# The start of a long kernel: inputs laid out in one run per partition, x squared by two engines, scale units before shift units, and ScalarE loads issued later

## The chip, the cores and the metric

The kernel runs on one core of a Trainium2 chip. The metric is the device time of one execution in microseconds, as the median of several. TensorE (PE) multiplies matrices, VectorE (DVE) and ScalarE (ACT) work elementwise, GpSimd (POOL) does a few elementwise steps and indirect transfers, SyncE (SP) issues most loads. Every engine runs its own list of instructions in order, and the lists meet at semaphores.

## The reference

The kernel computes one block of a model with attention, pooling and a mixture of experts, and then two layers of a second model. All is float32, with 512 tokens and a width of 1024. The change touches only the start of the first block:

```python
mod = jax.nn.silu(c) @ w_ada[l] + b_ada[l]               # c: one vector of 1024; w_ada: 1024 x 6144
sh1, sc1, g1, sh2, sc2, g2 = jnp.split(mod, N_MOD, axis=-1)
h = rms_norm(x, norm1_g[l]) * (1.0 + sc1[:, None]) + sh1[:, None]
z = h @ w_in[l]                                          # 1024 x 2048: q, k, v, u
```

So before the first large product there must be the root mean square of every token of x, the scale `sc1` and the shift `sh1`, and these two are products of one vector with the first 2048 columns of `w_ada`. Later come attention on q, k, v, window means (2, 4, 8, 16 wide) of u, and the experts.

## The kernel before

Nothing is planned by a compiler: each engine's list is written out by hand, and `take(engine, semaphore)` waits for a semaphore and clears it. Arrays are kept transposed, 128 channels on the partitions and 512 tokens along them, so x and h are 8 tiles of 128x512.

**Loads.** SP issues x (one transfer, 1024 rows of 2 KB) and then "units" of 2 MB into a ring of six slots (L1888 to L1891). A unit is 512 columns of a weight matrix with all 1024 rows, so it too is 1024 rows of 2 KB. Their order is w_ada 0, 1, 2, 3 (0 and 1 hold the shift, 2 and 3 the scale), w_in, w_ada 4, 5, w_in, w_ada 6, 7, and so on. A slot is refilled once its unit is used up. ACT issues the small parameters (`params_loaded`, L2329 to L2332) at the very start: a vector table, the constants, and a row broadcast to all partitions. After the fourth w_ada unit it issues the late constants, pool_w and the two router matrices (L2367 to L2370). POOL issues the inverse counts of the window means, `invcnt` (L1941), when all q and k are rotated (`qk_ready` 8).

**Mean square.** ACT squares the 8 tiles of x into two buffers `sq` in turn (L2343). PE sums each over its partitions with a product with ones (`sumsq`, L2040) and frees the buffer. ACT then takes the inverse root: a logarithm and an exponential, each with a table load (L2348, L2351).

**Scale and shift.** `mod_products` (L2057) makes the row of a w_ada unit: 8 products with a 32-column stationary tile, four of them side by side. ACT copies the row out of PSUM (`mod_moved`, L2357), and `mod_columns` (L2067) turns it into columns with four products of one moving column each, into bank 7. PE's list is: products 0, products 1, columns 0, products 2, columns 1, products 3, columns 2, columns 3. The w_ada units 4 to 11 are multiplied by DVE instead (`mod_unit`, L2604 and L2606), and PE turns them by `mod_columns` between the products of the projections.

**h and the projections.** DVE adds the bias (L2581), makes the gain (L2587, L2588) and scales x into hT (`normed`, L2593). ACT adds the shift tile by tile (L2374, semaphore `h_ready`). PE starts the first product of w_in (L2091) on the first tile. The projections of q and k (L2091), u (L2103) and v (L2115) follow without a pause. ACT copies each result (L2381, L2384, L2394, L2401), and DVE rotates q and k (L2616 to L2618), with a `mod_unit` after every second one. Then DVE waits for `invcnt` and makes the window means (L2629 to L2635) and `mod_unit` 8 to 11. PE needs the means at L2125, and w_ada unit 8 turned after the second product of v.

Of the kernel before, what the change touches and what calls it, by code (L numbers as in the profile page):

```python
# [17 lines left out]
ALU = mybir.AluOpType  # L18
# [3 lines left out]
P = 128  # L22
T = 512
D = 1024
# [18 lines left out]
POOL_W = (2, 4, 8, 16)  # L43
POOL_PAD = 8


P1 = {}
def _cols(table, spec):
# [40 lines left out]
def take(eng, sem, value=1):  # L89

    eng.wait_ge(sem, value)
    eng.sem_clear(sem)
# [39 lines left out]
        self.n = 0  # L132


def build(nc, xT_d, zero_row, par1, row1, cn, invcnt, w_ada, w_in, w_pool, w_out, w_rg, w_re, w_gate, w_up, w_down,
          w2, out):
    ctx = ExitStack()
    with ctx:
# [20 lines left out]
        for late, early in (("slot_full6", "wa_full"), ("slot_full7", "bonus_full"), ("slot_free6", "kr_full"),  # L159
                            ("slot_free7", "mla_q_full"), ("raw_tiles", "sg_full0"), ("tiles_used", "sg_full1")):  # L160
            sems[late] = sem(early)
        first_only = ("silu_c", "raw_ready", "v_ready", "u_ready", "qk_ready", "mix_ready", "x_mixed", "router_loaded",
                      "pool_w_loaded", "scores_done", "pooled", "params_loaded", "choices_full", "h_stored", "h_ready",
                      "x_loaded", "y_stored", "routed", "y_summed", "mod_ready", "rs_ready", "scaled", "pad_zero")
        for late, early in zip(("g_rk_full0", "g_rk_full1", "g_uw_free0", "g_uw_free1", "r_in_full", "r_bt_full", "r_k_free",
                                "r_bn_full", "r_k_done", "r_tok_full", "r_km_full", "r_func_full", "r_args_full", "r_sw_full",
                                "r_sa_full", "ring_free", "kk_full", "g_w_done", "x_tiles", "g_e_in0", "g_e_in1", "g_pt_full0",
# [141 lines left out]


        def ada_unit(n):
            return w_ada[0, :, n * 512:(n + 1) * 512].rearrange("(k p) n -> p k n", p=P)
        def in_unit(n):
            return w_in[0, :, n * 512:(n + 1) * 512].rearrange("(k p) n -> p k n", p=P)
        def out_unit(n):
            return w_out[0, :, n * 512:(n + 1) * 512].rearrange("(k p) n -> p k n", p=P)
        units = [ada_unit(n) for n in range(4)]
        ada_at, in_at = list(range(4)), []
        for n in range(4):
            in_at.append(len(units))  # L320
            ada_at += [len(units) + 1, len(units) + 2]
# [6 lines left out]
        def slot(n, k=8):  # L328
            return ring[:, n % SLOTS, :].rearrange("p (k n) -> p k n", k=k)
# [1555 lines left out]

        @block.sync
        def _(sp):
            sp.dma_start(xT[:], xT_d.rearrange("(k p) t -> p k t", p=P)).then_inc(sem("x_loaded"), 16)  # L1888
            for n, u in enumerate(units):
                take(sp, slot_free[n % SLOTS])  # L1890
                sp.dma_start(slot(n), u).then_inc(slot_full[n % SLOTS], 16)  # L1891
# [141 lines left out]
        def _(pe):  # L2033
# [26 lines left out]
            def mod_columns(u):  # L2060

                take(pe, sem(f"wT_full{u % 2}"))
                if u % 4 == 0:
                    take(pe, bank_free[7])
                for m in range(4):
                    col = 4 * (u % 4) + m
                    mm = pe.matmul(bank[7][:, col:col + 1], mod_rows[:, u % 2, m * P:(m + 1) * P],  # L2067
                                   quarters if u < 4 else ones[:, 0:1], start=True, stop=True)
                if u % 4 == 3:
                    mm.then_inc(for_dve[7], 1)  # L2070
                elif u >= 4:
                    mm.then_inc(sem(f"wT_free{u % 2}"), 1)

            sumsq(1, KD, 0)
            for u in range(4):
                mod_products(u)
                if u > 0:
                    mod_columns(u - 1)
            mod_columns(3)

            for n in range(2):
                s = in_at[n] % SLOTS
# [244 lines left out]
        def _(act):  # L2327
# [11 lines left out]
            def squares(src, tiles, n0=0):  # L2339
                for i in range(tiles):  # L2340
                    j = (n0 + i) % 2
                    take(act, sem(f"sq_free{j}"))
                    act.activation(sq[:, j, :], src(i), ACT.Square).then_inc(sem(f"sq_full{j}"), 1)  # L2343
# [15 lines left out]
                act.sem_inc(slot_free[ada_at[u] % SLOTS], 1)  # L2359
                act.sem_inc(sem(f"wT_full{u % 2}"), 1)  # L2360

            act.wait_ge(sem("x_loaded"), 16)
            squares(lambda i: xT[:, i, :], KD)
            inverse_root(1, 1.0 / D)
            for u in range(4):
                mod_moved(u)
            act.dma_start(c_sb[:, late_cols:], cn[:, late_cols:]).then_inc(sem("pool_w_loaded"), 16)  # L2367
            act.dma_start(pool_w[:], w_pool[0].rearrange("g c d -> c g d")).then_inc(sem("pool_w_loaded"), 16)
            act.dma_start(w_router[:, :, 0:4], w_rg[0].rearrange("(k p) n -> p k n", p=P)).then_inc(sem("router_loaded"), 16)
            act.dma_start(w_router[:, :, 4:36], w_re[0].rearrange("(k p) n -> p k n", p=P)).then_inc(sem("router_loaded"), 16)  # L2370
            act.wait_ge(sem("mod_ready"), 1)
            for k in range(KD):
                act.wait_ge(sem("scaled"), k + 1)
                act.activation(hT[:, k, :], hT[:, k, :], ACT.Identity, bias=mod[:, k:k + 1]).then_inc(sem("h_ready"), 1)  # L2374
            for i in range(8):
# [12 lines left out]
                if i % 4 == 3:  # L2388
                    act.sem_inc(slot_free[in_at[i // 4] % SLOTS], 1)
# [175 lines left out]
        def _(dve):  # L2565
# [8 lines left out]
            chain(dve.tensor_tensor(small[:, 20:21], small[:, 18:19], small[:, 19:20], ALU.subtract))  # L2574
            chain(dve.tensor_scalar(small[:, 21:22], small[:, 20:21], 0.2, None, ALU.add))
            chain(dve.tensor_scalar(subln, par("subln_g"), 0.8, None, ALU.mult))

            def modulation(first, b):
                take(dve, for_dve[b])
# [16 lines left out]
            def mod_unit(u):  # L2596
# [9 lines left out]
                        chain(dve.scalar_tensor_tensor(row, w, small[:, k:k + 1], row, ALU.mult, ALU.add))  # L2606
                dve.sem_inc(slot_free[s], 1)
                dve.sem_inc(sem(f"wT_full{u % 2}"), 1)
            modulation(0, 7)
            gains(0, par("norm1_g", 0, 8))  # L2610
            normed(0, 1)
            for i in range(8):
                dve.wait_ge(sem("raw_ready"), i + 1)
                if i == 0:
                    dve.wait_ge(sem("pool_w_loaded"), 32)
                chain(dve.tensor_tensor(qkT[:, i, :], raw[:, i % 2, :], const("cosA"), ALU.mult))  # L2616
                chain(dve.tensor_tensor(rtmp[:, i % 2, :], rot_raw[:, i % 2, :], const("sinA"), ALU.mult))
                dve.tensor_tensor(qkT[:, i, :], qkT[:, i, :], rtmp[:, i % 2, :], ALU.add).then_inc(sem("qk_ready"), 1)  # L2618
                if i % 2 == 1:
                    mod_unit(4 + i // 2)  # L2620
# [23 lines left out]
            dve.wait_ge(sem("router_loaded"), 32)  # L2644
# [437 lines left out]
```

## Time and profile before

| | us |
|---|---|
| median of 3 runs | 1996.08 (1995.02 to 1997.31) |
| profiled execution: span from first to last instruction | 2001.2 |
| PE busy | 1764.2 (88%) |
| DVE busy | 857.6 (43%) |
| ACT busy | 592.7 (30%) |

The profile page gives the profiled execution by its span, 2001.2 us, and no other time of it. The timed runs are other executions. All starts below are microseconds from the first instruction of the profiled execution. Float32 products show as two records each. A row of a timeline merges equal instructions that follow each other; what stands in brackets is the idle time before it and what ended it. Engine names with a q (ACTq, SPq) are the queue side of an engine: issued transfers and semaphore steps.

### The profile page before, as it was taken

The numbers are of one execution on the slowest core, as the hardware profiler recorded it, in microseconds if no ns is written. First come the engines' busy times: TensorE is split into PE (matmuls) and PEld (weight loads), VectorE is DVE, ScalarE is ACT, GpSimd is POOL, SyncE is SP. The second block draws the span as 40 slices with busy tenths as digits, with TensorE's granted clock in tenths as the row PEclk, the third lists the DMA queues.
The fourth block names the chain that finished last, engine by engine and source line by source line (L and its number), as shares of the span: only waits on it lengthen the run. The fifth ranks groups of instructions, "written<-read, shape, count | busy, mean of one in ns | idle before, by whom it ended". The sixth has DMA issues, their size and how long they took to land.

```text
span 2001.2 us, 44027 instructions
## 1 busy us (share of the span) xinstructions
PE 1764.2 (88%) x17970; PEld 1033.3 (52%) x17970; DVE 857.6 (43%) x1514; ACT 592.7 (30%) x1018; POOL 243.5 (12%) x270
## 2 busy tenths in 40 slices
PE   5998895977778877898999899999989998899996
PEld 2444543544444444445865784354447856853452
DVE  1567524111111111367666753151457747642331
ACT  3314521000000000334324424252253325424442
POOL 0002211111111111006112100001002103000001
PEclk8998996999999999998999999999999999999998
DMA  9758025999999999521000003110211000012101
GB/s 358 259 197 291 1 69 220 370 423 424 423 424 424 425 424 413 216 74 33 3 3 2 3 20 109 42 43 32 80 43 35 3 2 2 4 65 104 42 1 42
DMA packets 75098, 307.75 MB, mean 154 GB/s; under 512 B 10908, under 2 KB 22300, under 8 KB 57888
## 3 DMA queue, kind: packets, MB, share of 16 engines
q1 hardware_dynamic: 63280, 291.98, 37.2%
q0 software_dynamic: 5360, 9.33, 1.3%
q10 hardware_dynamic: 6272, 3.81, 0.6%
q8 instruction: 135, 2.21, 0.5%
q14 instruction: 51, 0.42, 0.1%
HBM read 301.01 MB, written 16.52 MB: 159 GB/s over the span
## 4 chain that ended last, share of the span: by engine, by line
PE 73%; DVE 13%; another core or an unknown queue 6%; ACT 4%; issue 3%; DMA 1%; DVEq 0%; ACTq 0%; POOL 0%; POOLq 0%
PE bank L2253 12%; PE bank L496 12%; PE bank L2269 6%; PE bank L1027 6%; PE bank L525 5%; PE bank L532 4%; PE bank L2091 3%; PE bank L2175 3%; PE bank L998 2%; DVE arena L1596 2%; ACT arena L1039 1%; PE bank L512 1%; PE bank L2115 1%; PE bank L2103 1%
## 5 line engine op out<-in xcount | busy, mean ns | idle before, releaser
L496 PE MATMUL bank<-hT,arena 128*128 128x512 f32 (+1 forms) x640 | 287.7, 605 | 3.6 <-ACTq L1040 2.4
L2253 PE MATMUL bank<-arena 128*64 128x256 f32 x1792 | 216.3, 399 | 66.9 <-remote 66.9
L525 PE MATMUL bank<-arena 64*64 64x64 f32 x6656 | 215.5, 220 | 22.7 <-DVE arena L1726 7.2
L525 PEld LDWEIGHTS bank<-arena 64*64 64x64 f32 x6656 | 203.8, 136 | 37.0 <-DVE arena L1726 10.1
L2253 PEld LDWEIGHTS bank<-arena 128*64 128x64 f32 x1792 | 135.6, 143 | 158.0 <-issue 107.8
L496 PEld LDWEIGHTS bank<-hT,arena 128*128 128x128 f32 (+1 forms) x640 | 122.9, 194 | 161.2 <-issue 156.6
L2859 DVE COPY arena<-bank 128x256 f32<-128x256 f32 x32 | 13.6, 425 | 329.6 <-PE bank L2261 329.6
L2269 PE MATMUL bank<-arena 128*64 128x512 f32 x448 | 104.0, 606 | 16.4 <-remote 16.4
L1027 PE MATMUL bank<-arena 128*128 128x512 f32 x256 | 110.4, 593 | 0.0
L1039 ACT ACTIVATE arena<-bank 128x512 f32<-128x512 f32 (+2 forms) x124 | 73.2, 590 | 118.9 <-PE bank L496 79.2
L532 PE MATMUL bank<-hT,arena 128*128 128x512 f32 x224 | 105.0, 607 | 1.7 <-remote 1.7
L2513 ACT ACTIVATE arena<-bank 128x512 f32<-128x512 f32 x32 | 19.1, 597 | 292.8 <-PE bank L2269 292.8
L1027 PEld LDWEIGHTS bank<-arena 128*128 128x128 f32 x256 | 48.5, 190 | 60.6 <-issue 60.1
L1852 DVE TENSOR_REDUCE arena<-bank 128x1 f32<-128x512 f32 x48 | 33.2, 692 | 106.0 <-PE bank L998 104.7
L2506 ACT ACTIVATE arena<-bank 128x256 f32<-128x256 f32 x32 | 12.3, 383 | 187.7 <-remote 187.7
L2269 PEld LDWEIGHTS bank<-arena 128*64 128x64 f32 x448 | 31.0, 138 | 69.7 <-issue 69.7
L512 PE MATMUL bank<-c_sb,arena 128*128 128x128 f32 x352 | 54.1, 288 | 12.8 <-ACTq L1040 7.9
L2091 PE MATMUL bank<-hT,arena 128*128 128x512 f32 x128 | 58.6, 619 | 5.3 <-ACT hT L2374 5.3
L532 PEld LDWEIGHTS bank<-hT,arena 128*128 128x128 f32 x224 | 39.8, 189 | 42.9 <-issue 41.2
L1986 POOL DMA_INDIRECT y_scratch<-arena x31 | 31.7, 1024 | 226.6 <-remote 205.9
L1176 ACT ACTIVATE arena<-bank 128x512 f32<-128x512 f32 x60 | 35.4, 597 | 80.2 <-PE bank L525 78.4
L512 PEld LDWEIGHTS bank<-c_sb,arena 128*128 128x128 f32 x352 | 40.4, 145 | 36.2 <-issue 36.0
(448 smaller groups left out, 2677.1 us busy)
## 6 DMA issues: line engine op xcount, KB each, us to landing
arena<-w_gate SPq DMA_DIRECT2D x28, 2048.0 KB, 30.6
arena<-w_up SPq DMA_DIRECT2D x28, 2048.0 KB, 21.0
arena<-w_down SPq DMA_DIRECT2D x28, 2048.0 KB, 26.2
arena<-w_ada SPq DMA_DIRECT2D x12, 2048.0 KB, 19.7
arena<-w_in SPq DMA_DIRECT2D x10, 2048.0 KB, 11.7
arena<-w_out SPq DMA_DIRECT2D x6, 2048.0 KB, 7.6
arena<-w_in SPq DMA_DIRECT2D x6, 1536.0 KB, 6.9
hT<-w_up SPq DMA_DIRECT2D x4, 2048.0 KB, 20.9
```

The source lines that it names most:

```text
L496: m = pe.matmul(bank[b][0:w, :], slot2(n)[:, k, c:c + w], hT[:, k, :], start=(k == 0), stop=(k == KD - 1))
L512: m = pe.transpose(bank[b][:, ts(t)], src[:, ts(t)], ident)
L525: m = pe.matmul(o[half(f), s, t], lhs[half(f), s, t], rhs[half(f), s, t], start=True, stop=True)
L532: m = pe.matmul(bank[b][:, :], slot2(3 + PLACE[i] // 4)[:, k, (PLACE[i] % 4) * P:(PLACE[i] % 4 + 1) * P], hT[:, k, :], start=(k == 0), sto ...
L998: pe.matmul(bank[i % 4][:, :], m_q[0:QK_M, h, ts(q)], m_k[0:QK_M, h, :], start=True, stop=True).then_inc(for_dve[i % 4], 1)
L1027: m = pe.matmul(bank[b][:, :], slot2(n)[:, k, (m_ % 4) * P:(m_ % 4 + 1) * P], mix[:, k, :], start=(i == 0), stop=(i == KD - 1))
L1039: chain(act.activation(dst, src, func, **kw))
L1596: dve.copy_predicated(blocks(g_T[d]), merged(d, l, False), blocks(bank[2 + d])).then_inc(sem(f"g_t_full{d}"), 1)
L2091: mm = pe.matmul(bank[b][:, :], slot(s)[:, k, m * P:(m + 1) * P], hT[:, k, :], start=(k == 0), stop=(k == KD - 1))
L2175: mm = pe.matmul(bank[4 + i % 4][:, :], slot(out_at + i // 4)[:, k, (i % 4) * P:(i % 4 + 1) * P], mixT[:, k, :], start=(n == 0), stop=(n = ...
L2253: mm = pe.matmul(bank[b][c * CAP:(c + 1) * CAP, 0:FE // 2], XT[j][:, k % 4, k // 4, :], e_slot(e_at(e, i), KD)[:, k, c * (FE // 2):(c + 1) ...
L2269: mm = pe.matmul(bank[6 + j][c * CAP:(c + 1) * CAP, :], hidT[:, j, f % 2, f // 2, :], e_slot(e_at(e, 2), 4)[:, f, c * HALF:(c + 1) * HALF] ...
```

## The change

- The host lays x out as two halves of 4 tiles, and each w_ada, w_in and w_out unit as one run of 16 KB per partition. pool_w and the router matrices (now one matrix) are also contiguous per partition. x is loaded in two transfers with a semaphore each.
- The first four units are w_ada 2, 3, 0, 1.
- ACT squares the even tiles of x into `sq` 0, DVE the odd ones into `sq` 1.
- PE's list is: products 2, columns 2, products 3, columns 3 (into bank 4), three products of ones with constants into bank 7 (`keep_busy`), products 0, columns 0, products 1, columns 1 (bank 7).
- DVE takes the scale from bank 4, makes the gains and hT, and then takes the shift from bank 7. ACT waits for both (`mod_ready` 2).
- ACT's transfers of late constants, pool_w and router stand behind its shift of h.

```diff
-        units = [ada_unit(n) for n in range(4)]
-        ada_at, in_at = list(range(4)), []
+        units = [ada_unit(n) for n in SCALE_FIRST]          # SCALE_FIRST = (2, 3, 0, 1)
+        ada_at, in_at = [SCALE_FIRST.index(n) for n in range(4)], []
...
-            sp.dma_start(xT[:], xT_d.rearrange("(k p) t -> p k t", p=P)).then_inc(sem("x_loaded"), 16)
+            for half in range(2):
+                sp.dma_start(xT[:, 4 * half:4 * half + 4, :], xT_d[half]).then_inc(sem(f"x_loaded{half}"), 16)
...
+            def keep_busy(n):
+
+                pe.wait_ge(bank_free[7], 1)
+                for _ in range(n):
+                    pe.matmul(bank[7][:, :], ones, c_sb[:, 0:512], start=True, stop=True)
             sumsq(1, KD, 0)
-            for u in range(4):
+            for u in SCALE_FIRST[:2]:
                 mod_products(u)
-                if u > 0:
-                    mod_columns(u - 1)
-            mod_columns(3)
+                mod_columns(u)
+            keep_busy(3)
+            for u in SCALE_FIRST[2:]:
+                mod_products(u)
+                mod_columns(u)
...
-            act.wait_ge(sem("x_loaded"), 16)
-            squares(lambda i: xT[:, i, :], KD)
+            for i in range(0, KD, 2):
+                if i % 4 == 0:
+                    act.wait_ge(sem(f"x_loaded{i // 4}"), 16)
+                take(act, sem("sq_free0"))
+                act.activation(sq[:, 0, :], xT[:, i, :], ACT.Square).then_inc(sem("sq_full0"), 1)
             inverse_root(1, 1.0 / D)
-            for u in range(4):
+            for u in SCALE_FIRST:
                 mod_moved(u)
-            act.dma_start(...)   # four transfers, two of them the router's
-            act.wait_ge(sem("mod_ready"), 1)
+            act.wait_ge(sem("mod_ready"), 2)
             for k in range(KD):
                 act.wait_ge(sem("scaled"), k + 1)
                 act.activation(hT[:, k, :], hT[:, k, :], ACT.Identity, bias=mod[:, k:k + 1]).then_inc(sem("h_ready"), 1)
+            act.dma_start(...)   # three transfers, one of them the router's
...
+            for i in range(1, KD, 2):
+                if i % 4 == 1:
+                    dve.wait_ge(sem(f"x_loaded{i // 4}"), 16)
+                take(dve, sem("sq_free1"))
+                dve.tensor_tensor(sq[:, 1, :], xT[:, i, :], xT[:, i, :], ALU.mult).then_inc(sem("sq_full1"), 1)
...
-            modulation(0, 7)
+            take(dve, for_dve[4])
+            chain(dve.tensor_tensor(mod[:, 8:16], bank[4][:, 8:16], par("b_ada", 8, 8), ALU.add))
+            dve.sem_inc(bank_free[4], 1)
+            dve.sem_inc(sem("mod_ready"), 1)
             gains(0, par("norm1_g", 0, 8))
             normed(0, 1)
+            shift_moved()        # the same for mod[:, 0:8] from bank 7
```

## Rows read from the trace of the kernel before

**Rows 1.** The page: busy time by engine.
```profile
PE 1764.2 (88%) x17970; PEld 1033.3 (52%) x17970; DVE 857.6 (43%) x1514; ACT 592.7 (30%) x1018; POOL 243.5 (12%) x270
```

**Rows 2.** The chain of waits, 0 to 60 us: start, length, what.
```profile
0.74 10.93 DMA xT<-xT_in
...
13.41 9.85 PE bank L2040 x16
23.26 3.57 PE bank L2057 x32
...
29.44 1.85 PE bank L2057 x16
...
36.67 3.52 PE bank L2067 x16
...
41.22 3.41 DVE hT L2593 x5
...
44.66 0.73 ACT hT L2374
...
45.44 14.77 PE bank L2091 x27
```

**Rows 3.** ACT's timeline, 5 to 45 us: start, length, instruction, idle before.
```profile
10.53 0.21 ACT L2334 ACTIVATE small<-p 128x8 f32<-128x8 f32 x1 [7.07 <-DMA r<-row]
...
20.26 0.63 ACT L2343 ACTIVATE sq<-xT 128x512 f32<-128x512 f32 x1 [0.30 <-PE bank L2040]
...
27.36 0.58 ACT L2357 ACTIVATE arena<-bank 128x512 f32<-128x512 f32 x1
...
31.45 0.60 ACT L2357 ACTIVATE arena<-bank 128x512 f32<-128x512 f32 x1 [2.58 <-PE bank L2057]
...
39.05 5.51 ACTq L2370 DMA_DIRECT2D w_router<-w_re  x1
```

**Rows 4.** PE's timeline, 28 to 48 us.
```profile
28.39 1.05 PE L2067 MATMUL bank<-c_sb,arena 128*128 128x1 f32 x8 [1.56 <-remote]
...
33.62 3.05 PE L2057 MATMUL bank<-arena,small 128*32 128x512 f32 x16 [1.34 <-remote]
```

**Rows 5.** Stretches: length, then busy time by engine, granted clock, DMA.
```profile
30.80:34.20 3.40, 2.06 (x24) 1.26 (x20) 0.00 (x0) 0.60 (x1) 0.00 (x0) 1.00 1.05 387
34.30:51.30 17.00, 11.74 (x35) 6.24 (x28) 5.90 (x11) 5.61 (x9) 0.00 (x0) 0.50 1.07 377
...
171.40:174.00 2.60, 0.00 (x0) 0.00 (x0) 2.42 (x5) 0.78 (x2) 0.00 (x0) 1.00 1.08 317
174.20:184.30 10.10, 9.44 (x22) 3.74 (x22) 7.23 (x15) 6.13 (x16) 4.68 (x3) 0.50 0.99 411
```

**Rows 6.** PE's timeline, 103 to 175 us.
```profile
127.48 7.11 PE L2103 MATMUL bank<-hT,arena 128*128 128x512 f32 x16
...
148.16 0.95 PE L2067 MATMUL bank<-c_sb,arena 128*128 128x1 f32 x8
```

**Rows 7.** DMA queues (q1 SP's, q10 ACT's), 47 to 53 us: packets, MB, share of 16 engines.
```profile
q1 hardware_dynamic: 1033, 2.08, 97.5%
q10 hardware_dynamic: 1036, 0.03, 12.5%
```

**Rows 8.** The same, 357 to 358.9 us, expert weights alone, 16 KB per packet.
```profile
q1 hardware_dynamic: 46, 0.75, 96.3%
```

**Rows 9.** The same, 114 to 121 us (q0 is POOL's).
```profile
q0 software_dynamic: 319, 1.05, 45.0%
```

**Rows 10.** DVE's timeline, 56 to 186 us.
```profile
65.67 0.69 DVE L2616 TENSOR_TENSOR arena<-arena,c_sb 128x512 f32<-128x512 f32 x1 [4.72 <-ACTq L2387]
...
121.71 0.71 DVE L2629 TENSOR_TENSOR arena<-arena 128x527 f32<-128x527 f32 x1 [5.00 <-DMA arena<-invcnt]
...
135.53 0.71 DVE L2629 TENSOR_TENSOR arena<-arena 128x527 f32<-128x527 f32 x1 [3.65 <-ACTq L2396]
...
141.74 5.47 DVE L2606 SCALAR_TENSOR_TENSOR arena<-arena,small 128x512 f32<-128x512 f32 x7
```

More of the change, by code:

```diff
@@ L44 @@
 POOL_PAD = 8
+SCALE_FIRST = (2, 3, 0, 1)
 P1 = {}
@@ L132, in reset, with build @@
         self.n = 0
-def build(nc, xT_d, zero_row, par1, row1, cn, invcnt, w_ada, w_in, w_pool, w_out, w_rg, w_re, w_gate, w_up, w_down,
+def build(nc, xT_d, zero_row, par1, row1, cn, invcnt, w_ada, w_in, w_pool, w_out, w_r, w_gate, w_up, w_down,
           w2, out):
@@ L161, in build @@
             sems[late] = sem(early)
-        first_only = ("silu_c", "raw_ready", "v_ready", "u_ready", "qk_ready", "mix_ready", "x_mixed", "router_loaded",
+        first_only = ("silu_c", "raw_ready", "x_loaded1", "u_ready", "qk_ready", "mix_ready", "x_mixed", "router_loaded",
                       "pool_w_loaded", "scores_done", "pooled", "params_loaded", "choices_full", "h_stored", "h_ready",
-                      "x_loaded", "y_stored", "routed", "y_summed", "mod_ready", "rs_ready", "scaled", "pad_zero")
+                      "x_loaded0", "y_stored", "routed", "y_summed", "mod_ready", "rs_ready", "scaled", "pad_zero")
         for late, early in zip(("g_rk_full0", "g_rk_full1", "g_uw_free0", "g_uw_free1", "r_in_full", "r_bt_full", "r_k_free",
@@ L311, in ada_unit @@
         def ada_unit(n):
-            return w_ada[0, :, n * 512:(n + 1) * 512].rearrange("(k p) n -> p k n", p=P)
+            return w_ada[n]
         def in_unit(n):
-            return w_in[0, :, n * 512:(n + 1) * 512].rearrange("(k p) n -> p k n", p=P)
+            return w_in[n]
         def out_unit(n):
-            return w_out[0, :, n * 512:(n + 1) * 512].rearrange("(k p) n -> p k n", p=P)
-        units = [ada_unit(n) for n in range(4)]
-        ada_at, in_at = list(range(4)), []
+            return w_out[n]
+        units = [ada_unit(n) for n in SCALE_FIRST]
+        ada_at, in_at = [SCALE_FIRST.index(n) for n in range(4)], []
         for n in range(4):
@@ L1887, in _ @@
         def _(sp):
-            sp.dma_start(xT[:], xT_d.rearrange("(k p) t -> p k t", p=P)).then_inc(sem("x_loaded"), 16)
+            for half in range(2):
+                sp.dma_start(xT[:, 4 * half:4 * half + 4, :], xT_d[half]).then_inc(sem(f"x_loaded{half}"), 16)
             for n, u in enumerate(units):
                 take(sp, slot_free[n % SLOTS])
-                sp.dma_start(slot(n), u).then_inc(slot_full[n % SLOTS], 16)
+                sp.dma_start(ring[:, n % SLOTS, :], u).then_inc(slot_full[n % SLOTS], 16)
             sp.dma_start(y_d, zero_row.to_broadcast([2 * T, D])).then_inc(sem("y_loaded"), 16)
@@ L2062, in mod_columns @@
                 take(pe, sem(f"wT_full{u % 2}"))
-                if u % 4 == 0:
-                    take(pe, bank_free[7])
+                b = 4 if u in SCALE_FIRST[:2] else 7
+                if u % 4 == 0 or u == SCALE_FIRST[0]:
+                    take(pe, bank_free[b])
                 for m in range(4):
                     col = 4 * (u % 4) + m
-                    mm = pe.matmul(bank[7][:, col:col + 1], mod_rows[:, u % 2, m * P:(m + 1) * P],
+                    mm = pe.matmul(bank[b][:, col:col + 1], mod_rows[:, u % 2, m * P:(m + 1) * P],
                                    quarters if u < 4 else ones[:, 0:1], start=True, stop=True)
-                if u % 4 == 3:
-                    mm.then_inc(for_dve[7], 1)
+                if u % 4 == 3 or u == SCALE_FIRST[3]:
+                    mm.then_inc(for_dve[b], 1)
                 elif u >= 4:
                     mm.then_inc(sem(f"wT_free{u % 2}"), 1)
+            def keep_busy(n):
+                pe.wait_ge(bank_free[7], 1)
+                for _ in range(n):
+                    pe.matmul(bank[7][:, :], ones, c_sb[:, 0:512], start=True, stop=True)
             sumsq(1, KD, 0)
-            for u in range(4):
+            for u in SCALE_FIRST[:2]:
                 mod_products(u)
-                if u > 0:
-                    mod_columns(u - 1)
-            mod_columns(3)
+                mod_columns(u)
[3 more added lines that the diff above has]
+                mod_columns(u)
             for n in range(2):
@@ L2360, in mod_moved @@
                 act.sem_inc(sem(f"wT_full{u % 2}"), 1)
-            act.wait_ge(sem("x_loaded"), 16)
-            squares(lambda i: xT[:, i, :], KD)
+            for i in range(0, KD, 2):
[3 more added lines that the diff above has]
+                act.activation(sq[:, 0, :], xT[:, i, :], ACT.Square).then_inc(sem("sq_full0"), 1)
             inverse_root(1, 1.0 / D)
-            for u in range(4):
+            for u in SCALE_FIRST:
                 mod_moved(u)
[L2367 to L2370, printed above, removed]
-            act.wait_ge(sem("mod_ready"), 1)
+            act.wait_ge(sem("mod_ready"), 2)
             for k in range(KD):
@@ L2374, in _ @@
                 act.activation(hT[:, k, :], hT[:, k, :], ACT.Identity, bias=mod[:, k:k + 1]).then_inc(sem("h_ready"), 1)
+            act.dma_start(c_sb[:, late_cols:], cn[:, late_cols:]).then_inc(sem("pool_w_loaded"), 16)
+            act.dma_start(pool_w[:], w_pool).then_inc(sem("pool_w_loaded"), 16)
+            act.dma_start(w_router[:], w_r).then_inc(sem("router_loaded"), 16)
             for i in range(8):
@@ L2608, in mod_unit, with shift_moved @@
                 dve.sem_inc(sem(f"wT_full{u % 2}"), 1)
-            modulation(0, 7)
+            take(dve, for_dve[4])
+            chain(dve.tensor_tensor(mod[:, 8:16], bank[4][:, 8:16], par("b_ada", 8, 8), ALU.add))
+            dve.sem_inc(bank_free[4], 1)
+            dve.sem_inc(sem("mod_ready"), 1)
             gains(0, par("norm1_g", 0, 8))
+            def shift_moved():
+                take(dve, for_dve[7])
+                chain(dve.tensor_tensor(mod[:, 0:8], bank[7][:, 0:8], par("b_ada", 0, 8), ALU.add))
+                dve.sem_inc(bank_free[7], 1)
+                dve.sem_inc(sem("mod_ready"), 1)
             normed(0, 1)
+            shift_moved()
             for i in range(8):
@@ L2643, in _ @@
             gains(1, par("norm2_g", 0, 8))
-            dve.wait_ge(sem("router_loaded"), 32)
+            dve.wait_ge(sem("router_loaded"), 16)
             def over_cols(v):
@@ L3070, in col, with by_units @@
         return np.asarray(a).reshape(-1, P).T
+    def by_units(w):
+        w = np.asarray(w)[0]
+        return w.reshape(KD, P, -1, 512).transpose(2, 1, 0, 3).reshape(-1, P, KD * 512)
     par1 = np.concatenate([col(norm1_g), col(b_ada), col(norm2_g), col(final_g), col(pool_scale), col(subln_g), col(c),
@@ L3076 @@
     out = nc.dram_tensor("out", (D, T), F32, kind="ExternalOutput").ap()
-    build(nc, put("xT_in", np.asarray(x)[0].T), put("zero_row", np.zeros((1, D), np.float32)), put("par1", par1), put("row1", row1), put("cn", cn), put("invcnt", ic),
-          put("w_ada", w_ada), put("w_in", np.asarray(w_in)[..., rotary_columns()]), put("w_pool", w_pool), put("w_out", w_out), put("w_rg", w_router_group),
-          put("w_re", w_router_expert), put("w_gate", w_gate), put("w_up", w_up), put("w_down", w_down), second_inputs({**rest, "final_norm_g_2": final_norm_g_2}, put), out)
+    build(nc, put("xT_in", np.asarray(x)[0].T.reshape(2, 4, P, T).transpose(0, 2, 1, 3)), put("zero_row", np.zeros((1, D), np.float32)), put("par1", par1), put("row1", row1), put("cn", cn), put("invcnt", ic),
+          put("w_ada", by_units(w_ada)), put("w_in", by_units(np.asarray(w_in)[..., rotary_columns()])),
+          put("w_pool", np.asarray(w_pool)[0].transpose(1, 0, 2)), put("w_out", by_units(w_out)),
+          put("w_route", np.concatenate([np.asarray(w_router_group)[0], np.asarray(w_router_expert)[0]], axis=1).reshape(KD, P, 36).transpose(1, 0, 2)),
+          put("w_gate", w_gate), put("w_up", w_up), put("w_down", w_down), second_inputs({**rest, "final_norm_g_2": final_norm_g_2}, put), out)
     r = run_bass_kernel_spmd(nc, [arrays], core_ids=[0])
```

## The prediction

> **What bounds the kernel now.** I read the page first, then the chain of waits of the first 60 us, then the timelines of PE, ACT and DVE there, the stretches with their granted clock, and last the DMA queues. The page shows PE as the bound: it is busy for 88% of the span [rows 1]. The change touches the stretch before PE's long run, so what counts is when the first projection starts and how fast it then goes. The chain shows what that start hangs on: x arrives at 11.67, the sums of squares run from 13.41 to 23.26, products and columns of the four w_ada units end at 40.19, and the projection starts at 45.44 [rows 2]. Two of these pieces are not what they seem. The wait for x is not the last one: ACT and DVE are held until the broadcast row of parameters lands at 10.53, and from there to ACT's first square it is 2.1 us of small work [rows 3]; x has come by then. And from 40.39 on the last link is ACT's own list. It issues the router matrix for 5.51 us, until 44.56, and can only then add the shift [rows 3], though DVE had the first tile ready at about 42.0 (it began its tiles at 41.22, five in 3.41 us [rows 2]). The clock is the third piece: PE ran at 1.2 GHz from 34.3 to 51.3 (granted 0.50), after a stretch in which it was busy for 2.06 of 3.40 us, half of this with one-column products [rows 4, 5].
>
> **Parameters: 0 us.** Packets of 16 KB of the expert weights took 1.9 x 16 x 0.963 / 46 = 0.64 us each [rows 8]. Where SP's and ACT's queues were both full, they sent packet for packet: 1033 against 1036 [rows 7]. The constants and the row are 128 pieces each, 16 per DMA engine, so after the change they go in turn with sixteen packets of 8 or 16 KB. With 8 KB at half of 0.64 and small ones at 0.1 that is 13 x 0.42 + 3 x 0.74 = 7.7 us from about 3 us on, landing at 10.7 against 10.53. If they start before x they land near 9 (-1.5); if mostly behind 16 KB packets, 3 us later. I take 0. x itself, with 16 packets per engine, still is not last.
>
> The Trainium skill (DMA: Bandwidth & Descriptors, Queues, rings and completion order) says that a DMA engine drains a whole packet of some 9 to 17 descriptors from one ring before it turns to the next. By that rule the row would wait for about one packet of x and land near 9.5, and the stall priced below for `invcnt` would shrink to under 1 us. The near equal counts in [rows 7] speak for one by one, and I go by them.
>
> **Squares: 0 us.** ACT needs 0.63 us a tile, PE 0.86, so ACT was not the limit. Each of the two buffers goes round: PE's product, release, square, product. ACT's idle 0.30 us, ended by PE [rows 3], is this round, and it stays with DVE as the second squarer: its elementwise product of 512 columns takes 0.69 us [rows 10], 0.06 more. I bound it by half a us on both sides. So sums end at 23.3 as before.
>
> **New order of units: +0.2 us if the clock stays full.** From the end of the sums to the first columns PE must wait for ACT's inverse root, with its two table loads, and one copy: 28.39 - 23.26 = 5.13 us [rows 2, 4]. Before, two products filled 3.6 of it; now only one does, as the columns stand ahead of the second product. One unit in the new order is products 1.85 [rows 2], end of products to copy 0.15, copy 0.60 [rows 3], copy to columns 0.45 (27.94 to 28.39), columns 1.05 [rows 4]: 4.1 us with nothing beside it. So columns of the fourth unit end at 23.26 + 5.13 + 1.05 + 3 x 4.1 = 41.7, and the three products of `keep_busy` add 3 x 0.86 = 2.6 (a 16-record group of eight takes 7.0 to 7.1 us [rows 6], 0.87 each). From 44.3 it is 1.3 us to the projection (DVE's add, semaphores, ACT's 0.73 tile): 45.6 against 45.44. The scaling of x, 5.4 us of DVE, lies beside the shift's units and goes off the path; the w_ada units arrive ahead of need, which removes the 1.34 us wait at 33.62 [rows 4], and ACT's 5.51 us issue is gone. All of it is paid back by the serial order. ACT's moved transfers are three instead of four and are queued behind the shift, ahead of its copies of q. The late constants are what DVE's first rotation needs, 13 us after the start of the projection; the shift is done 5 us after that start and they land at worst 10 us later, 8 turns of 0.64 + 0.17 us for them and as many for pool_w. The 2 us that this may be late are covered by the 4.72 us that DVE was idle before its second rotation [rows 10]; without it they would be paid.
>
> **The clock in the new order: +4.9 us.** After products of the first unit PE now stands idle for about 3.3 us, then does one-column work. Rows show twice what follows: at 30.8 to 34.2 PE was busy for 2.06 us with the clock full, then it fell; at 171.4 to 174.0 it was idle, then it fell for 10 us [rows 5]. I expect it to fall by 28 us. At 1.2 GHz the 16 one-column products took 3.52 us instead of 2.1 [rows 2], so 0.75 more per unit; products 1.85 more; `keep_busy` 2.6 more. It rose again at 51.3 after the projection had run for 5.9 us [rows 5], so `keep_busy` mostly raises it only at its own end. Second unit 1.85 + 0.75, `keep_busy` 2.6 less 0.3 for an early rise: 4.9, and the projection starts at 50.5. Bounds: 0 if it never falls; if it stays low to the end, two more units, 4 x 1.3 = 5.2 more (10.4).
>
> **The clock in the projection: -1.0 us.** Before, 45.44 to 51.3 ran at half speed, a loss of 2.9 us [rows 5]. After `keep_busy` come again two units with pauses, so I expect a low clock near the start, but a shorter one. Ends: 0 and -2.9.
>
> **invcnt: +1.7 us.** POOL's 256 pieces of 4 KB were sent between 114 and 121 [rows 9], beside three 2 MB units in 2 KB packets. Now these units are 24 packets of 0.64 us per DMA engine, issued at 108.8 and running until 126; POOL's 16 per engine go in turn with them, 16 x (0.64 + 0.17) = 13 us from 114.5: landing near 128 instead of 121.7. DVE waits for them (5.00 us before, some 6.3 more). It then has 3.65 us of waiting for ACT that absorb it [rows 10], so the last window mean and `mod_unit` 8 come some 2.6 us later. That one ended at 147.2, PE needed it at 148.16 [rows 6, 10]: 0.9 us of slack, so PE loses 1.7. Ends: 0 (it is sent before the big packets) and +3.
>
> **Sum.** 0 + 0 + 0.2 + 4.9 - 1.0 + 1.7 = +5.8 us. The later stages shift as a whole: expert weights wait for free slots, which free with the work. The sum is against the profiled span, 2001.2, which lies 5.1 above the median of the runs; carried over as a difference it gives 1996.1 + 5.8 = 2001.9. All lower ends together: -1.5 - 0.5 + 0.2 - 2.9 = -4.7; all upper: 3 + 0.5 + 0.2 + 10.4 + 0 + 3 = +17, which needs everything at once.
>
> **The rivals.** (a) As forecast, 0.52: +2.5 to +9. (b) The other side: the clock is full through the units and in the projection, 0.20. Its place is the pause after the first products; its price is all of the 4.9 and the 2.9 that the projection lost before: 0.2 - 2.9 + 1.7 = -1.0, 1995.1, with 2 us to either side. It decides if the projection starts before about 47 with a granted clock of 1.00. For it: PE's pauses up to 30.8 left the clock full, and it came back at 184.3 after scattered work of attention [rows 5]. Against: this pause is longer than any of these. (c) Small transfers do not go one by one behind the large ones, 0.15: the parameters land 1 us earlier and `invcnt` costs nothing, 5.8 - 1 - 1.7 = +3.1, 1999.2. For it: nothing here shows 16 KB packets beside ACT's queue. Against: [rows 7]. It is what the rule of the Trainium skill named above would bring. (d) The parameters are stuck behind 16 KB packets, 0.13: 5.8 + 3 = +8.8, 2004.9, seen as a first square near 15.7 instead of 12.65. For it: the large transfers are issued within microseconds of each other. Against: p, constants and row are issued as early.
>
> **Chances.** Within 0.2% is within 4 us, about what a measurement of this kernel can tell from no change. Slower by more: 0.39 of (a), 0.04 of (c), all of (d): 0.56. Same: 0.13 of (a), 0.11 of (b), 0.09 of (c): 0.33. Faster: 0.09 of (b), if it comes with less than the stall for `invcnt`, and 0.02 of (c): 0.11. The range 1994.5 to 2006.5 takes in (c), two thirds of (b) and most of (d); outside lie about 0.08 below and 0.10 above.
>
> **What would show it.** In the changed profile: the first square near 12.7; ACT and DVE idle before squares, ended by PE; PE idle for 3 us after the first products; a granted clock of 0.50 from about 28 to 40; the projection's start near 50; the wait for `invcnt` at 10 us or more; a PE wait of 1 to 2 us at the columns of unit 8. I am wrong if the projection starts before 46, or if the clock is full through the units.

## The result: 1% slower, and where the 20 us went

| | before | after |
|---|---|---|
| median, us (4 runs each) | 1996.22 | 2015.78 (2014.5 to 2018.28) |
| ratio, 95% interval | | 1.0104 (1.0082 to 1.0125) |
| span of the profiled execution, us | 2001.2 | 2012.7 |

The direction was forecast, the size was not: +5.8 us (2001.9) were expected and +19.6 us came, 9 us above the upper end of the range (2006.5). One execution of the kernel before, among those run beside the experiments below, took 9078 us and is left out.

The spans differ by 11.5 us only. That is an accident of the two profiled executions. The stages behind the second attention scores are the same code, but took 1827.1 us before and 1819.0 after, and the one of before ran longer at half clock (from 200 us on its mean granted clock is 0.97, that of after 0.98). The view of cores shows the mean over the whole span, first of before, then of after:

```profile
core 0: 2001.2 us, clock 0.964
```

```profile
core 0: 2012.7 us, clock 0.971
```

So I compare stage by stage, up to the second group of attention scores, which both kernels reach by the same path. Before it started at 174.07 (the end of the idle stretch in [rows 5]), after at 193.74: 19.7 us later, which is the measured difference. From PE's timelines, first the start of the v product and of these scores before, then the scores after:

```profile
134.43 13.90 PE L2115 MATMUL bank<-arena,hT 128*128 128x512 f32 x32
174.07 5.35 PE L2137 MATMUL bank<-arena 64*128 64x512 f32 x8 [2.69 <-ACTq L2424]
```

```profile
193.74 5.07 PE L2148 MATMUL bank<-arena 64*128 64x512 f32 x8 [3.07 <-ACTq L2437]
```

Now the chain of waits of the kernel after, 0 to 70 us, which answers to [rows 2]:

```profile
1.67 13.83 DMA r<-row
...
18.41 9.59 PE bank L2043 x14
...
28.04 1.12 PE bank L2043 x2
29.16 1.85 PE bank L2060 x16
31.01 3.19 another core or an unknown queue
...
34.29 1.86 PE bank L2071 x8
36.15 3.65 PE bank L2060 x16
...
40.80 1.86 PE bank L2071 x8
42.66 5.33 PE bank L2082 x6
47.99 1.85 PE bank L2060 x16
...
57.35 12.69 PE bank L2102 x25
```

The chain now begins with the broadcast row instead of x. PE's pause of 3.19 us after the first products is plain to see, and behind it columns take 1.86 us, products 3.65 and `keep_busy` 5.33: all at half clock. The stretches show the clock itself (length, busy time by engine, granted clock, DMA):

```profile
24.10:34.10 10.00, 6.87 (x26) 1.61 (x24) 1.39 (x2) 5.59 (x7) 0.00 (x0) 1.00 0.99 424
34.30:47.80 13.50, 12.42 (x38) 5.91 (x38) 4.69 (x10) 0.60 (x1) 0.00 (x0) 0.50 1.00 427
48.00:58.00 10.00, 6.44 (x50) 3.03 (x51) 1.17 (x3) 2.62 (x5) 0.00 (x0) 1.00 0.70 257
58.20:61.50 3.30, 3.30 (x5) 1.35 (x4) 0.00 (x0) 3.30 (x6) 0.00 (x0) 0.50 0.96 372
...
164.00:170.70 6.70, 6.63 (x14) 3.89 (x15) 5.91 (x9) 0.00 (x0) 0.00 (x0) 0.50 0.88 325
```

It fell at the end of the pause, came back only when `keep_busy` was over, and fell once more for 3.4 us at the start of the projection. The last row is a half-clock stretch that before did not exist. Its cause stands in the timelines of DVE and PE, which answer to [rows 10] and [rows 6]:

```profile
141.74 0.71 DVE L2656 TENSOR_TENSOR arena<-arena 128x527 f32<-128x527 f32 x1 [14.34 <-DMA arena<-invcnt]
```

```profile
145.12 13.90 PE L2126 MATMUL bank<-arena,hT 128*128 128x512 f32 x32
164.06 1.86 PE L2071 MATMUL bank<-c_sb,arena 128*128 128x1 f32 x8 [5.05 <-remote]
165.79 9.59 PE L2126 MATMUL bank<-arena,hT 128*128 128x512 f32 x16
```

DVE waits 14.34 us for `invcnt` instead of 5.00. PE then idles 5.05 us before the columns of w_ada unit 8 and does these and most of the next v product at half clock.

| piece | before | after | difference | forecast |
|---|---|---|---|---|
| row of parameters lands | 10.53 | 15.52 | +5.0 | 0 |
| landing to start of the sums | 2.9 | 2.9 | 0 | 0 |
| sums of squares | 9.85 | 10.75 | +0.9 | 0 |
| end of the sums to first projection | 22.2 | 28.2 | +6.0 | +5.1 |
| q, k and u projections | 89.0 | 87.8 | -1.2 | -1.0 |
| start of v to second scores | 39.6 | 48.6 | +9.0 | +1.7 |
| sum | | | +19.7 | +5.8 |

### The profile page after: what moved, and what is told of

Read it like the earlier page. It is cut to its first block, busy times and chain, and to the rows that moved or that the text cites. A ratio compares the mean times of both kernels' runs of the same rounds, so it can differ in the third digit from the quotient of the medians.

```text
span 2012.7 us, 44046 instructions
## 1 busy us (share of the span) xinstructions
PE 1760.7 (87%) x17976; PEld 1028.1 (51%) x17976; DVE 861.0 (43%) x1519; ACT 590.4 (29%) x1014; POOL 243.9 (12%) x270
## 4 chain that ended last, share of the span: by engine, by line
PE 73%; DVE 12%; another core or an unknown queue 6%; ACT 4%; issue 3%; DMA 1%; DVEq 0%; ACTq 0%; POOL 0%; POOLq 0%
PE bank L498 12%; PE bank L2264 12%; PE bank L2280 6%; PE bank L1029 5%; PE bank L527 5%; PE bank L534 4%; PE bank L2102 3%; PE bank L2186 3%; PE bank L1000 2%; DVE arena L1598 2%; ACT arena L1041 2%; PE bank L514 2%; PE bank L2126 1%; PE bank L2114 1%
## 5 line engine op out<-in xcount | busy, mean ns | idle before, releaser
L514 PEld LDWEIGHTS bank<-c_sb,arena 128*128 128x128 f32 x352 | 40.0, 144 | 36.4 <-issue 36.1
```

Source lines behind the costliest of these rows:

```text
L514: m = pe.transpose(bank[b][:, ts(t)], src[:, ts(t)], ident)
```

## The experiments

Two theories stood against each other. Theory 1: small transfers take turns with the packets of SP's queue, one for one, so the new 16 KB packets delay the parameters and `invcnt`, and the order of the units is a third, separate cost. Theory 2: PE's new order costs nearly everything and the layout nothing. The kernel before was run beside each of the three batches: 1995.8, 1995.3 and 1996.8 us. The kernel after was not, it has the four runs above. Single executions of one kernel spread over 10 to 15 us here, so I take a median to be good to about 2 us, and positions in the profile carry more weight. A profile is of one execution, though: those of row_layout, params_first, inv_apart, no_busy and paired_act_squares are the fastest of their runs.

| kernel | median us | ratio to before, 95% | row or last parameter lands | projection starts | DVE's wait for invcnt |
|---|---|---|---|---|---|
| row_layout | 2000.59 | 1.0016 to 1.0043 | 9.66 | 47.45 | 5.53 |
| layout_alone | 2006.01 | 1.0035 to 1.0074 | 15.47 | 46.76 | 14.33 |
| params_first | 2006.37 | 1.0046 to 1.0092 | 7.09 | 49.29 | 14.31 |
| inv_apart | 2008.04 | 1.0049 to 1.0092 | 15.51 | 53.30 | 3.14 |
| both_fixed | 2000.53 | 1.0005 to 1.0036 | 6.86 | 48.46 | 3.04 |
| no_busy | 1999.06 | 1.0002 to 1.0023 | 6.88 | 43.72 | 3.07 |
| paired | 1992.61 | 0.9967 to 0.9993 | 6.72 | 39.18 | 3.33 |
| paired_act_squares | 1988.18 | 0.9952 to 0.9980 | 7.00 | 38.78 | 3.37 |
| one_run_params | 2008.78 | 1.0036 to 1.0079 | 7.19 | 48.98 | 14.32 |
| one_run_inv | 2007.00 | 1.0037 to 1.0067 | 15.51 | 57.58 | 7.03 |
| best | 1987.71 | 0.9937 to 0.9971 | 7.46 | 37.96 | 3.28 |
| transfers_ahead | 1988.22 | 0.9941 to 0.9973 | 7.51 | 37.64 | 3.00 |

**row_layout**: the change without its layout of x and the units. The cut shows w_ada; x, w_in and w_out go back to 2 KB rows in the same way.

```diff
-            return w_ada[n]
+            return w_ada[0, :, n * 512:(n + 1) * 512].rearrange("(k p) n -> p k n", p=P)
```

> The changed kernel with x and the w_ada, w_in, w_out units again in 2 KB rows; all else of the change stays. Theory 1 (small transfers take turns with the units' packets, so 16 KB packets delay the parameters by 5 us and invcnt by some 13 us): the row lands near 10.5 instead of 15.5, DVE waits about 5 us for invcnt, PE does not stall at the columns of unit 8; the projection starts near 52, and the time is about 2015.8 - 5 - 9 = 2002. Theory 2 (the new order of the units costs nearly all of it, the layout nothing): the time stays above 2012.

Measured 2000.59, 15 us back. The row lands at 9.66 and the stall at unit 8 is gone. The projection started earlier than expected, 47.45, since the clock came back at about 33.8 this time, before the second unit's columns and so before `keep_busy`. Its timeline of PE:

```profile
34.36 1.05 PE L2071 MATMUL bank<-c_sb,arena 128*128 128x1 f32 x8 [1.08 <-ACTq L2371]
...
148.94 0.95 PE L2071 MATMUL bank<-c_sb,arena 128*128 128x1 f32 x8
```

The first row is the second unit's columns, 1.05 us instead of 1.86. The second is unit 8: no idle stretch stands before its columns, and they take 0.95 us, full clock.

**layout_alone**: the kernel before, with the layouts only.

> The kernel before with the new layouts alone (units and x in one run per partition, x in two transfers with one semaphore, pool_w and one router matrix contiguous), old order, squares by ACT, ACT's transfers ahead of the shift. Theory 1: the row lands at 15.5, the sums start at 18.4, but the units no longer hold PE and ACT's issue is short, so the projection starts about 16 us after the sums, near 44.5; DVE waits 14 us for invcnt and PE loses 8 to 9 us there; time about 1996.2 - 1 + 9 = 2004. Theory 2: nothing is lost, 1995 or below.

Measured 2006.01. The layout costs 10 us by itself. ACT's and DVE's views show the same two delays as in the kernel after, to 0.1 us, with the old order of units:

```profile
15.47 0.21 ACT L2335 ACTIVATE small<-p 128x8 f32<-128x8 f32 x1 [12.04 <-DMA r<-row]
```

```profile
132.00 0.71 DVE L2629 TENSOR_TENSOR arena<-arena 128x527 f32<-128x527 f32 x1 [14.33 <-DMA arena<-invcnt]
```

Theory 2 falls with it. The projection starts at 46.76, 2.3 us later than I expected, though the sums start 4.95 us later than before: the units' landing no longer holds PE, and ACT's issue is short. That hides most of the first delay, but none of the second.

**params_first**: parameters issued by SP ahead of x.

```diff
+            sp.dma_start(p1[:], par1).then_inc(sem("params_loaded"), 16)
+            sp.dma_start(r1[:], row1.to_broadcast([P, N_R1])).then_inc(sem("params_loaded"), 16)
+            sp.dma_start(c_sb[:, 0:early], cn[:, 0:early]).then_inc(sem("params_loaded"), 16)
             for half in range(2):
```

> The changed kernel with the three parameter transfers issued by SP ahead of x instead of by ACT beside it. Theory 1: they land near 5 to 6 us, the sums start near 9 when the first half of x is there, 9 us earlier than 18.4, and all of it comes back: about 2007. Theory 2: the start is covered by the w_ada units, less than 2 us come back.

Measured 2006.37. They land at 7.09, and the sums start at 10.45 instead of 18.41. Now x is last, with 0.36 us of ACT's wait. I had expected the start of the sums 1.5 us earlier, but the time is as forecast.

**inv_apart**: w_ada units 10 and 11 held for `invcnt`.

```diff
                 take(sp, slot_free[n % SLOTS])
+                if n == 14:
+                    sp.wait_ge(sem("inv_loaded"), 64)
```

> The changed kernel with SP holding back w_ada units 10 and 11 (units 14 and 15 of its list) until invcnt has landed. Theory 1: DVE's wait for invcnt falls from 14.3 to 5 us or less, PE's stall of 5.05 us at the columns of unit 8 and the half clock behind it vanish: 2015.8 - 9 = 2007. Rival: the stall comes from DVE's own work or from the units held back, and 2 us or less come back.

Measured 2008.04. DVE's wait is 3.14 us, PE's stall is gone, and from the start of v to the second scores it is 40.0 us (141.07 to 181.09) instead of 48.6. The projection also started 4 us earlier than in the kernel after, at 53.30; that is the clock, which came back before the second columns as in row_layout, and not this edit.

```profile
126.49 0.71 DVE L2658 TENSOR_TENSOR arena<-arena 128x527 f32<-128x527 f32 x1 [3.14 <-DMA arena<-invcnt]
```

**one_run_params** and **one_run_inv** ask what makes a small transfer slow beside large packets: its bytes, or the number of its pieces. Both move the same bytes as the kernel after, in fewer pieces.

```diff
-            act.dma_start(p1[:], par1).then_inc(sem("params_loaded"), 16)
-            act.dma_start(c_sb[:, 0:late_cols], cn[:, 0:late_cols]).then_inc(sem("params_loaded"), 16)
-            act.dma_start(r1[:], row1.to_broadcast([P, N_R1])).then_inc(sem("params_loaded"), 16)
+            act.dma_start(prc[:, 0:early_cols], par1).then_inc(sem("params_loaded"), 16)
```

```diff
-            for g in range(4):
-                pool.dma_start(inv_c[:, g, :], invcnt[g:g + 1, :].to_broadcast([P, T])).then_inc(sem("inv_loaded"), 16)
+            pool.dma_start(probs.rearrange("p a c n -> p (a c n)"), invcnt).then_inc(sem("inv_loaded"), 16)
```

> The changed kernel with vector table, broadcast row and early constants laid side by side by the host and loaded by ACT in one transfer: the same 0.49 MB in 128 pieces instead of 384, 8 per DMA engine instead of 24. Theory 1 (small transfers wait piece by piece, one packet of the other queue each): 8 turns of some 0.45 us, landing near 7 instead of 15.5, the sums start near 10 with x, 8 us come back: about 2008. Rival (the queues share the bytes evenly, pieces do not matter): landing above 13, 2 us or less come back.

> The changed kernel with invcnt replicated by the host and loaded by POOL in one transfer of 128 pieces of 8 KB, the same 1 MB, instead of four transfers in 320 packets. Theory 1: 9 turns of 0.9 us instead of 20 of 0.77: DVE's wait falls from 14.3 to about 7.5 us, PE's stall of 5 us and the fall of the clock behind it go: about 2009. Rival (bytes are shared): the wait stays at 13 us or more and so does the time.

Measured 2008.78 and 2007.00, both as theory 1 has it; in one_run_inv PE's stall is gone too. The timelines of ACT and of DVE:

```profile
7.19 0.21 ACT L2343 ACTIVATE small<-prc 128x8 f32<-128x8 f32 x1 [4.72 <-DMA prc<-par]
```

```profile
134.66 0.71 DVE L2655 TENSOR_TENSOR arena<-arena 128x527 f32<-128x527 f32 x1 [7.03 <-DMA arena<-invcnt]
```

A third of the pieces brings the parameters in at 7.19 instead of 15.52. It is the pieces that wait, one packet of the other queue each. The queues of one_run_params from 3.5 to 4.0 us show it without any sum: 17 packets of 8 KB and 16 pieces of the parameters, about one of each for each of the 16 DMA engines.

```profile
q1 hardware_dynamic: 17, 0.14, 65.8%
q10 hardware_dynamic: 16, 0.06, 31.2%
```

In both runs the host also writes the broadcast values out for every partition, so these reads come from a larger array. No run separates that.

**both_fixed** joins params_first and inv_apart; **no_busy** is the same without `keep_busy(3)`.

> The changed kernel with both cures: SP issues the parameters ahead of x, and holds w_ada units 10 and 11 until invcnt has landed. What stays is the new order of the units. Theory 1 (three separate costs that add up): 2015.8 - 9 - 8 = 1998.5, the projection starts near 49 when the clock stays low through keep_busy, near 46 when it rises in it. Rival (the cures share one wait): 2004 or more.

> both_fixed without the three products of keep_busy (their result is never read). Theory 1: they stand on the path with 2.7 us at full clock and 5.3 at half, and the clock falls in spite of them, so without them the projection starts 2 to 3 us earlier, though with the clock at half for longer: time 0 to 3 us below both_fixed. Rival (keep_busy earns its time by the clock): 2 us or more above both_fixed.

Measured 2000.53 and 1999.06. The two cures together bring back 15 us. Both_fixed is still 5.3 us above the kernel before although its sums start 3.2 us earlier (10.22); what is left of the change is the order of the units and the squares on DVE, which the next two runs take apart. In its profile the projection starts at 48.46 and the attention at 176.25, 2.2 us after that of before. The medians of the two differ by 1.5 us, which these runs can't tell from nothing; in the profiles the projection starts 4.7 us earlier without `keep_busy`, at 43.72, but then runs its first 5 us at half clock. Part of the 4.7 us is chance: in no_busy the clock came back at 31.6, before the second columns, with no `keep_busy` to raise it. `keep_busy` earns nothing here that shows; that it costs is likely and not shown by the times.

**paired** is both_fixed with PE's old interlocked order:

```diff
-            for u in SCALE_FIRST[:2]:
-                mod_products(u)
-                mod_columns(u)
-            keep_busy(3)
-            for u in SCALE_FIRST[2:]:
-                mod_products(u)
-                mod_columns(u)
+            mod_products(2)
+            mod_products(3)
+            mod_columns(2)
+            mod_products(0)
+            mod_columns(3)
+            mod_products(1)
+            mod_columns(0)
+            mod_columns(1)
```

> both_fixed with PE's old interlocked order, scale units first: products 2, 3, columns 2, products 0, columns 3, products 1, columns 0, 1, and no keep_busy. Theory 1: products fill the waits for ACT. Sums end near 20, the last unit lands near 29, and the projection starts near 35 to 37, some 12 us before both_fixed: 1986 to 1988, below both kernels. Rival (the start hangs on the units' landing or on the clock, not on PE's order): 1995 or more.

Measured 1992.61, faster than before by 0.1 to 0.3%, and 8 us below both_fixed. PE's timeline shows two units' products (x32) ahead of the pause, which is now 1.55 us, and columns of 1.05 us: the clock stayed full until 32.6.

```profile
20.80 3.64 PE L2066 MATMUL bank<-arena,small 128*32 128x512 f32 x32
25.98 1.05 PE L2077 MATMUL bank<-c_sb,arena 128*128 128x1 f32 x8 [1.55 <-remote]
26.96 1.92 PE L2066 MATMUL bank<-arena,small 128*32 128x512 f32 x16
28.82 1.05 PE L2077 MATMUL bank<-c_sb,arena 128*128 128x1 f32 x8
31.66 2.74 PE L2066 MATMUL bank<-arena,small 128*32 128x512 f32 x16 [1.79 <-remote]
```

The start, 39.18, is 2 to 4 us later than I expected, and the time 4.6 us above the upper end of the expectation. The fourth unit lands at 31.6, not 29 (the idle 1.79 us), and behind it the clock fell at 32.6, so the last two sets of columns took 3.58 us (34.33 to 37.91) instead of about 2.2. DVE had finished its scaling at 36.2 and waited for them.

**paired_act_squares** gives all squares back to ACT.

> paired with all eight squares by ACT, as in the kernel before. Theory 1: the sums go by the round of each buffer (product, release, square), not by ACT, so they take within 0.5 us of paired's. Rival (ACT's squares were the limit): 1.5 us longer or more.

The sums take 10.01 us against 10.60 in paired, and the time is 1988.18 against 1992.61. It is not worse. Whether the squares on DVE cost something stays open: in both profiles the first products of the sums run at about half their later rate, until about 15.6 in paired and 14.9 here, and that alone differs from execution to execution (see below). That ACT's squares were the limit is refuted.

**best** and **transfers_ahead**: parameters in one run, inv_apart, paired order, ACT's squares; the second with ACT's transfers ahead of the shift again.

> What the runs so far point to: run-per-partition layouts, parameters in one run, SP holding w_ada units 10 and 11 for invcnt, PE's interlocked order with scale units first, squares by ACT. Theory 1: the sums start near 10, the fourth unit lands near 30 and ends the wait, the projection starts at 37 to 38: 1986 to 1988. Rival (the earlier sums are not hidden): 1984 or less.

> best with ACT's three transfers ahead of the wait for the shift, as in the kernel before. Theory 1: contiguous, they need some 1.6 us of ACT's queue in a time when ACT is idle anyway, so the time is within 2 us of best; the 5.51 us of the kernel before were the router matrix in 128-byte pieces. Rival (the place was what mattered): 4 us slower or more.

Measured 1987.71 and 1988.22, both below both kernels (0.3 to 0.6% below before). The place of ACT's transfers makes no difference, as transfers_ahead's timeline of ACT says: three issues of 0.46 us or less, in a time when ACT waits for DVE anyway.

```profile
33.02 0.36 ACTq L2382 DMA_DIRECT2D prc<-cn  x1
33.41 0.46 ACTq L2383 DMA_DIRECT2D pool_w<-w_pool  x1
33.89 0.45 ACTq L2384 DMA_DIRECT2D w_router<-w_route  x1
36.87 5.00 ACT L2388 ACTIVATE hT<-hT,mod 128x512 f32<-128x512 f32 x8 [4.09 <-DVEq L2632]
```

So of the 5.51 us in [rows 3] the layout of the router matrix was the cause, not the place. What ends the start now is DVE's scaling; its timeline in best:

```profile
31.54 5.39 DVE L2607 SCALAR_TENSOR_TENSOR hT<-xT,gs,rs 128x512 f32<-128x512 f32 x8
36.85 0.16 DVE L2630 TENSOR_TENSOR mod<-bank,prc 128x8 f32<-128x8 f32 x1
```

The row at 36.85 adds the shift's bias, and DVE comes to it only behind all eight tiles. In best the shift's columns were done by about 36.1, in transfers_ahead, where the clock stayed full, by 34.2, with the bias at 36.52. Taking the bias up between two tiles would by these rows let the start come some 0.6 to 2.2 us earlier (an estimate). It was not tried.

## Why the prediction was wrong

**Parameters: mis-sized, 0 forecast, +5.0 measured.** The mechanism was in the text, packet for packet from [rows 7], and holds: between 3 and 15 us the kernel after sent 419 packets of SP's queue and 418 of ACT's.

```profile
q1 hardware_dynamic: 419, 4.22, 87.7%
q10 hardware_dynamic: 418, 0.50, 13.5%
```

What failed is the count of turns. I took 16 pieces per DMA engine and left out the vector table's 8, and the small packet that each transfer sends at its end on each engine: 24 + 3 = 27 turns in all (ACT's queue sent 432 packets up to 40 us), 418 / 16 = 26 of them in these 12 us. By bytes, 4.22 MB in 419 packets are about 16 packets of 8 KB, 8 of 16 KB and 2 small ones per engine. With the prices of the prediction that gives 16 x 0.42 + 8 x 0.74 = 12.6 us, from about 3 to 15.6, where 12.5 were measured: the prices hold, the count did not. Rival (d), with 0.13, comes nearest: the late first square was its sign. But I had it at +3 with a first square at 15.7, and it came at 17.64; of the 10 turns that I had not counted, about half met packets of 16 KB.

```profile
17.64 0.61 ACT L2377 ACTIVATE sq<-xT 128x512 f32<-128x512 f32 x1
```

The rule of the Trainium skill that I weighed against it (DMA: Bandwidth & Descriptors, Queues, rings and completion order: a DMA engine drains a packet of some 9 to 17 descriptors before it turns to the next ring) does not hold for these transfers. By it, as the prediction estimated, the row would have come near 9.5; it came at 15.52. Equal counts over 12 us would not exclude long turns, but the half microsecond of one_run_params above shows one packet of each queue per engine, and both runs with fewer pieces follow the count of pieces. Rival (c) falls with it.

**invcnt: mis-sized, +1.7 forecast, +9.0 measured.** Three parts. First the turns again: I counted 16 per engine, and there are 20, for [rows 9] shows 319 packets and not 256 (four transfers with an end packet on each of 16 engines). Between 126 and 140 the kernel after sent:

```profile
q1 hardware_dynamic: 302, 4.23, 71.8%
q0 software_dynamic: 314, 1.03, 21.4%
```

So DVE's wait grew by 9.3 us instead of 6.3. A turn took 14 x 16 x (0.718 / 302 + 0.214 / 314) = 0.69 us, less than the 0.81 of the prediction, but POOL's first piece went out only at about 126, 4 us after its issue at 121.80. Second, the slack was nearly right: 9.3 less 3.65 and 0.9 is 4.8, and PE idled 5.05. Third, what I had left out altogether: the idle stretch cost PE its clock. Columns 1.86 instead of 0.95, the v product 9.59 instead of 7.11, and 0.4 more before the scores: 3.8 us. A stall before dense work was priced at its length when it costs more. In inv_apart, where the stall is gone, 8.6 us of this stage come back, and in both_fixed and one_run_inv it takes the same 40.0 us.

**New order and clock of the units: right, +5.1 forecast, +6.0 measured.** The clock fell 5.1 us after the end of the sums (34.3), where I had it at 4.7 (28), and stayed low until `keep_busy` was over. I had only the second unit's columns slow; both sets were. In row_layout and inv_apart, with the same order, it rose already before the second columns, and `keep_busy` then took 2.68 us and not 5.3. So the stretch from the end of the sums to the projection took 24.8 us in two profiles and 28.0 to 28.2 in five for the same instructions, a spread that lies within the bounds. Rival (b), a full clock, showed in none of the seven profiles with this order and `keep_busy`.

**Squares: nearly right, 0 forecast, +0.9 measured.** The round of the two buffers is what sets the sums: in the kernel after both ACT and DVE idle before each square but their first, ended by PE. Most of the 0.9 us is the slow start of the products. Groups of PE's records, from 18 to 21 and from 25 to 28 us of the kernel after (mean ns of one):

```profile
L2043 PE MATMUL bank<-sq,c_sb 128*128 128x512 f32 x3 | 2.9, 1113 | 18.4 <-ACT sq L2377 18.4
L2043 PE MATMUL bank<-sq,c_sb 128*128 128x512 f32 x6 | 3.1, 640 | 0.0
```

The slow part lasted to about 24 here, 5 to 6 us, and to about 17 before, some 4 us. The granted clock reads 1.00 in both parts, so these rows do not say whether it is the clock. With ACT alone the sums took 9.46 to 10.77 us in five profiles, with the split 10.17 to 10.97 in nine.

**Projection: right, -1.0 forecast, -1.2 measured. Transfers behind the shift: right,** they are worth nothing beside the new order, and DVE's first rotation came at 69.50 with no wait for them.

## What to carry to other kernels

Count the pieces of every small transfer that runs beside a queue of large ones, all of them, with the end markers: each waits for one packet of the other queue, and an eightfold packet makes an urgent small transfer late though the total rate rises (387 GB/s in [rows 5], 424 to 427 in the stretches after). Cure the small transfer (one run per partition, or issue it ahead), or hold the large ones back, before making their packets large. On an in-order PE, work that needs a round trip through another engine wants independent products behind it; a pause there costs its length, and the pauses of 3.3 us and more in these profiles also cost the clock.

## What the runs showed of the hardware

Where two queues were both full, packets went nearly one for one at every size met here: 1033 to 1036 in [rows 7], 419 to 418 for pieces of 372 bytes to 2.4 KB against 8 and 16 KB, 302 to 314 for pieces of 4 KB against 16 KB. The same 0.49 MB of parameters landed at 7.19 us in one transfer and at 15.52 in three. The granted clock fell to 1.2 GHz during or right behind the pause of 3.3 us that follows the first unit's products (at 34.3 in the kernel after, with no column product before it), and it fell at 34.2 before and at 58.2 after, behind stretches of short pauses and 1.05 to 2 us of products with one moving column. These runs do not tell the pauses from the columns as the cause of the last two. Whether the clock came back before or behind `keep_busy` changed from one execution to the next: inv_apart and the kernel after have the same instructions up to there, and it came back at about 39.7 and 47.9. And the same program differs by 14 us from execution to execution with one core alone: the kernel before took 1988.25 us at a mean granted clock of 0.975 and 2002.42 at 0.965.
